# Memory keys and values of a two-part model made inside the expert loop, late norms' squares summed on GpSimd

## The reference

```python
def memory_cross_attention(h, mem_n, wq, wkv, wo, q_gain, k_gain):
    q = rms_norm((h @ wq).reshape(B_, T, X_HEADS, X_HEAD_DIM), q_gain)      # 4 heads of 256
    k, v = jnp.split(mem_n @ wkv, 2, axis=-1)
    k = rms_norm(k.reshape(B_, M, X_HEADS, X_HEAD_DIM), k_gain)
    ...
    return o @ wo
# in each layer l of the second block
x = x + 0.5 * swiglu(rms_norm(x, norm_ffn1[l]), ...)
x = x + concat(mixers of rms_norm(x, norm_mix[l])) @ w_out[l]
x = x + memory_cross_attention(rms_norm(x, norm_cross[l]), rms_norm(mem, norm_mem[l]), ...)
x = x + 0.5 * swiglu(rms_norm(x, norm_ffn2[l]), ...)
```

## Time and profile before

| | us |
|---|---|
| median of 3 runs (lowest, highest) | 3019.21 (3018.96, 3020.18) |
| the profiled execution | 3018.08 |
| its span, first to last instruction | 3016.5 |
| TensorE busy (matmul), share | 2541.1, 84% |
| VectorE, ScalarE, GpSimd busy | 1261.3, 874.6, 41.6 |
| read from DRAM, written | 659.21 MB, 1.05 MB |

### The profile page before, as it was taken

The page is one execution under the profiler, slowest core; times in us unless marked ns, Lnnn a source line. Parts: engine busy times, 40 slices in busy tenths (PEclk is TensorE's granted clock), DMA queues, the critical chain, the costliest instruction groups (busy, mean ns, idle before and its releaser), DMA issues.

```text
span 3016.5 us, 42653 instructions
## 1 busy us (share of the span) xinstructions
PE 2541.1 (84%) x18068; PEld 1984.1 (66%) x18068; DVE 1261.3 (42%) x1844; ACT 874.6 (29%) x1213; POOL 41.6 (1%) x52
## 2 busy tenths in 40 slices
PE   6898788666766767676999698989999997899999
PEld 6895384122212222223999587989999985888999
DVE  6665532000000000002656745655565566465555
ACT  3473021000000000002444422544444444144443
POOL 0000000000000000000000100000000001000000
PEclk9998897878777787777999788989999997899999
DMA  6443056999999999997554201425555540033453
GB/s 224 141 144 116 1 199 277 426 424 426 426 425 424 426 426 424 425 426 298 202 182 161 84 1 57 168 84 183 182 189 183 181 161 1 15 112 112 143 184 122
DMA packets 115400, 662.49 MB, mean 220 GB/s; under 512 B 10283, under 2 KB 12502, under 8 KB 57777
## 3 DMA queue, kind: packets, MB, share of 16 engines
q1 hardware_dynamic: 113376, 650.24, 55.4%
q0 software_dynamic: 1872, 10.06, 1.0%
HBM read 659.21 MB, written 1.05 MB: 219 GB/s over the span
## 4 chain that ended last, share of the span: by engine, by line
PE 60%; DMA 17%; DVE 10%; SPq 5%; DVEq 3%; ACT 3%; issue 2%; ACTq 0%; PEldq 0%; PEld 0%
PE psd L548 32%; PE psx L548 8%; DMA ring<-in_w_up 7%; SPq L2172 5%; DMA hx<-in_w_down 5%; DMA ring<-in_w_down 5%; PE psd L795 2%; PE psd L786 2%; PE psx L823 2%; PE psx L962 2%; DVE w_lo L1462 2%; PE psd L814 1%; DVE scr L1462 1%; PE psx L558 1%; PE psx L706 1%
## 5 line engine op out<-in xcount | busy, mean ns | idle before, releaser
L548 PE MATMUL psd<-h_hi,w_hi 128*128 128x256 f32 x2704 | 779.9, 288 | 43.8 <-DVE h_lo L1462 20.5
L548 PE MATMUL psd<-h_lo,w_hi 128*128 128x256 f32 x2704 | 773.4, 286 | 0.0
L548 PE MATMUL psd<-h_hi,w_lo 128*128 128x256 f32 x2704 | 773.0, 286 | 0.0
L1462 DVE TENSOR_TENSOR w_lo<-ring,w_hi 128x1024 fp32r<-128x1024 f32 (+1 forms) x468 | 550.1, 1217 | 492.3 <-ACT w_hi L1132 489.7
L1132 ACT ACTIVATE w_hi<-ring 128x1024 fp32r<-128x1024 f32 (+1 forms) x468 | 467.5, 1047 | 389.1 <-PE psd L548 383.7
L548 PEld LDWEIGHTS psd<-h_hi,w_hi 128*128 128x128 f32 x2704 | 527.8, 195 | 50.3 <-issue 24.7
L548 PEld LDWEIGHTS psd<-h_lo,w_hi 128*128 128x128 f32 x2704 | 527.7, 195 | 0.5
L548 PEld LDWEIGHTS psd<-h_hi,w_lo 128*128 128x128 f32 x2704 | 527.5, 195 | 0.0
L548 PE MATMUL psx<-halves,w_hi 128*128 128x256 f32 x1408 | 256.9, 284 | 3.2 <-issue 3.2
L548 PEld LDWEIGHTS psx<-halves,w_hi 128*128 128x128 f32 x1408 | 219.9, 192 | 4.2 <-issue 3.9
L1125 ACT ACTIVATE scr<-psd 128x512 f32<-128x512 f32 x56 | 33.2, 592 | 606.8 <-PE psd L801 316.8
(11 more groups left out here) (331 smaller groups left out, 3084.3 us busy)
## 6 DMA issues: line engine op xcount, KB each, us to landing
ring<-in_ffn_wi SPq DMA_DIRECT2D x88, 1024.0 KB, 4.8
scr<-in_w_gate SPq DMA_DIRECT2D x48, 1024.0 KB, 18.8
scr<-in_w_down SPq DMA_DIRECT2D x48, 1024.0 KB, 22.3
scr<-in_w_up SPq DMA_DIRECT2D x48, 1024.0 KB, 26.7
ring<-in_ffn_wo SPq DMA_DIRECT2D x44, 1024.0 KB, 4.8
ring<-in_w_gate SPq DMA_DIRECT2D x32, 1024.0 KB, 17.8
ring<-in_w_up SPq DMA_DIRECT2D x32, 1024.0 KB, 25.5
ring<-in_w_down SPq DMA_DIRECT2D x32, 1024.0 KB, 23.3
```

Of the source, the lines that this page charges most:

```text
L548: mm = pe.matmul(o, w[u], a[v], start=start and i == 0, stop=stop and i == 2, **kw)
L1462: return dve.tensor_tensor(o, a, b, op)
```

## The change

It does three things. The keys and values of both layers are made in the expert loop, one slot of `x_wkv` an expert: expert e of round `pair` makes slot `pair` of layer e; slots 0 to 3 are keys, 4 to 7 values. The matmuls are plain fp32 (16 a slot). Keys are normed in the loop. Results are stored to a DRAM tensor `kv` by ScalarE's queue and loaded again by GpSimd's queue in each layer. The memory is loaded, squared, summed and normed once, ahead of and at the start of the loop, mostly on GpSimd; `mem_n` lies in the buffers of x and sq, which are free during the loop. Second, `norm_cross` becomes a late norm, and both it and `norm_ffn2` are early. Third, the squares of late norms are summed by three adds on GpSimd from 8 tiles to 2, so TensorE does 2 matmuls.

```diff
# plan: x_k and x_v are gone, x_q is evicted by VectorE
-        after += [(("x_k", l), i, "x_wkv", (l, i)) for i in range(4)]
-        after += [(("x_v", l), i, "x_wkv", (l, 4 + i)) for i in range(4)]
# TensorE: norm, when g is a late norm
+                if g in SUMMED:
+                    pe.wait_ge(squares_summed, SUMMED.index(g) + 1)
+                    for k in range(2):
+                        mm = pe.matmul(b[:, 0:T], ones, squares_of.get(g, sq)[:, k, :], start=(k == 0), stop=(k == 1))
+                    done(mm)
+                    return
# TensorE: ffn's last step
-                                if g and dt in (3, 5):
-                                    norm(g, dt // 2 - 1, dt // 2)
# TensorE: expert, between the turns and "down"
                 pe.wait_ge(S("actT"), 2 * pair + e + 1)
+                pe.wait_ge(S("mem_normed"), 1)
+                pe.wait_ge(S("kv_w_landed"), 32 * pair + 16 * e + 16)
+                w = kv_w.rearrange("p (k c) -> p k c", k=KD)
+                for m in range(2):
+                    tile = slice(m * P, (m + 1) * P)
+                    for k in range(KD):
+                        a, b = (w[:, k, tile], mem_n[e][:, k, :]) if keys else (mem_n[e][:, k, tile], w[:, k, :])
+                        mm = pe.matmul(m2(psd[0])[:, m, :], a, b, start=(k == 0), stop=(k == KD - 1))
+                mm.then_inc(S("kv_made"), 1)
...
+                if keys:
+                    pe.wait_ge(S("k_squared"), 2 * pair + e + 1)
+                    for m in range(2):
+                        mm = pe.matmul(psd[1][:, 0:T], ones, k_sq[:, m, :], start=(m == 0), stop=(m == 1))
+                    mm.then_inc(S("k_summed"), 1)
                 pe.wait_ge(S("ye_ready"), 4 * pair + 2 * e + 2)
...
+                pe.wait_ge(S("kv_read"), 2 * pair + e + 1)
+                if keys:
+                    pe.wait_ge(S("k_root"), 2 * pair + e + 1)
# TensorE: cross-attention, after mix_out
                 for i in range(4):
-                    dense((("x_k", l), i), (mn_hi, mn_lo), f"norm_mem{l}" if i == 0 else None)
-                    if i == 1:
+                    dense((("x_q", l), i), (mn_hi, mn_lo), g=f"norm_cross{l}" if i == 0 else None)
+                    if i == 0:
                         norm(f"norm_cross{l}")
# TensorE: after cross-attention
-                then_norm(("x_o", l), f"norm_ffn2{l}", ("xo_cut", 4 * l), last=2)
-                ffn("ffn2", l, f"norm_ffn1{l + 1}" if l < LAYERS - 1 else None)
+                for i in range(4):
+                    dense((("x_o", l), i), (mn_hi, mn_lo), ready=None if i else ("xo_cut", 4 * l))
+                ffn("ffn2", l)
# ScalarE: expert, after actT
+                    act.wait_ge(S("kv_made"), 2 * pair + e + 1)
+                    if keys:
+                        act.activation(k_sq, m2(psd[0]), ACT.Square).then_inc(S("k_squared"), 1)
+                    act.wait_ge(S("kv_stage_free"), 32 * pair + 16 * e + 16)
+                    copy(kv_st, psd[0][:, :]).then_inc(S("kv_read"), 1)
                     act.wait_ge(slots_done, PAIR * pair + first + ESLOTS)
                     copy(ye[:, 0, :], psd[2][:, :]).then_inc(S("ye_ready"), 1)
+                    if keys:
+                        act.wait_ge(S("k_summed"), 2 * pair + e + 1)
+                        act.activation(k_rs, psd[1][:, 0:T], ACT.Sqrt, bias=eps_col,
+                                       scale=1.0 / 256).then_inc(S("k_root"), 1)
+                        act.wait_ge(S("k_scaled"), 2 * pair + e + 1)
...
+                    act.dma_start(kv[e, bass.ds(pair, 1), :, :].rearrange("a p c -> (a p) c"),
+                                  kv_st).then_inc(S("kv_stage_free"), 16)
# VectorE: x_q is multiplied by rstd; k_scaled: reciprocal of k_rs and two products in each key expert
+                for i in range(4):
+                    cut_ahead(cutter, (("x_q", l), i))
+                    b = m2(d_ready(dve, (("x_q", l), i)))
+                    dread(tt_(xq[:, 2 * i:2 * i + 2, :], b, by_token, ALU.mult))
# GpSimd
+            def sum_squares(g):
+
+                s, q = squares_of.get(g, sq), 4 * NORMS.index(g)
+                pool.wait_ge(sq_ready, q + 2)
+                pool.tensor_tensor(s[:, 0:2, :], s[:, 0:2, :], s[:, 2:4, :], ALU.add)
+                pool.wait_ge(sq_ready, q + 4)
+                pool.tensor_tensor(s[:, 4:6, :], s[:, 4:6, :], s[:, 6:8, :], ALU.add)
+                pool.drain()
+                pool.tensor_tensor(s[:, 0:2, :], s[:, 0:2, :], s[:, 4:6, :], ALU.add)
+                pool.drain().then_inc(squares_summed, 1)
...
+            load(mem[:, :, :], A["memT"].rearrange("(k p) t -> p k t", p=P), "mem_in")
+            DB.was_read(pool, ("w_b_out", 3))
...
+            for l in range(LAYERS):
+                for k in range(KD):
+                    pool.tensor_scalar(mem_n[l][:, k, :], mem[:, k, :], pc(f"norm_mem{l}", k), None, ALU.mult)
# SyncE, in the expert loop
                     expert_slot(s, pair)
+                    if s == 16 + ERING - 1:
+                        sp.wait_ge(S("kv_made"), 2 * pair + 1)
+                        kv_slot(1, pair)
+                    if s == ESLOTS + 16 + ERING - 1:
+                        sp.wait_ge(S("kv_made"), 2 * pair + 2)
+                        kv_slot(0, pair + 1)
```

More of the change, by code:

```diff
@@ L207, in dense_plan @@
         ffn(l, "ffn1")
-        for part, count, reader in (("mix_in", 11, "dve"), ("mix_out", 4, "dve"), ("x_k", 4, "act"),
-                                    ("x_v", 4, "act"), ("x_q", 4, "act"), ("x_o", 4, "dve")):
+        for part, count, reader in (("mix_in", 11, "dve"), ("mix_out", 4, "dve"), ("x_q", 4, "dve"),
+                                    ("x_o", 4, "dve")):
             plan += [(((part, l), i), reader) for i in range(count)]
@@ L246, in small_plan @@
     add("act", "norm", "g_ffn")
+    add("act", "norm_mem")
     add("dve", "router")
@@ L453, in program @@
         for l in range(LAYERS):
-            NORMS += [f"norm_ffn1{l}", f"norm_mix{l}", f"norm_mem{l}", f"norm_cross{l}", f"norm_ffn2{l}"]
+            NORMS += [f"norm_ffn1{l}", f"norm_mix{l}", f"norm_cross{l}", f"norm_ffn2{l}"]
         sq_ready, h_ready = S("sq_ready"), S("h_ready")
@@ L738, in _ @@
             then_norm("w_o", "g_ffn", ("merged", 0), (mn_hi, mn_lo))
+            b = XB.claim(pe, ("norm_mem",))
+            pe.wait_ge(S("mem_squared"), 1)
+            for i in range(2):
+                mm = pe.matmul(b[:, 0:T], ones, mem_sq[:, 0, i, :], start=(i == 0), stop=(i == 1))
+            done(mm)
             b = XB.claim(pe, ("router",))
@@ L778, in down_rows, with expert @@
                 return e_ring[s % ERING].rearrange("p (i c) -> p i c", i=2)
-            def expert(pair, e):
+            def expert(pair, e, keys):
                 first = e * ESLOTS
@@ L833, in _ @@
             for l in range(LAYERS):
-                if l == 0:
-                    norm(f"norm_ffn1{l}", 0, 2)
-                ffn("ffn1", l, f"norm_mix{l}")
+                ffn("ffn1", l)
                 for i in range(9):
@@ L1055, in _ @@
                 for i in range(4):
-                    dense((("x_k", l), i), (mn_hi, mn_lo), f"norm_mem{l}" if i == 0 else None)
-                    if i == 1:
+                    dense((("x_q", l), i), (mn_hi, mn_lo), g=f"norm_cross{l}" if i == 0 else None)
+                    if i == 0:
                         norm(f"norm_cross{l}")
[L1059 to L1080, removed]
                 b = XB.claim(pe, ("xnorm", l, "q", 0))
                 for hd in range(4):
-                    pe.wait_ge(S("x_sq"), 8 * l + 4 + hd + 1)
+                    pe.wait_ge(S("x_sq"), 4 * l + hd + 1)
                     for it in range(TT):
@@ L1175, in norm, with late_norm @@
                     cut_acts(h, hi, mid=mid)
-            def late_norm(g, part, l, first, early, each=None):
+            def late_norm(g, part, l, first, early, each=None, hi=h_hi):
                 for i in range(4):
@@ L1294, in _, with expert @@
                     read(copy(h_tok[:, tt, i * 512:(i + 1) * 512], b[:, :]))
-            with act.Fori(0, EXPERTS // 2) as pair:
-                for e in range(2):
+            act.drain().then_inc(S("kv_stage_free"), 16)
+            def expert(pair, e, keys):
                     first = MOE + e * ESLOTS
@@ L1791, in _, with expert @@
             dve.drain().then_inc(S("onehot"), 1)
-            def expert(pair, e):
+            XB.was_read(dve, ("norm_mem",))
+            dve.reciprocal(rmem, rmem).then_inc(S("mem_root"), 1)
+            for l in range(LAYERS):
+                tt_(k_gain[:, l, :], *(par[:, PCOL[f"x_{n}_gain{l}"]:PCOL[f"x_{n}_gain{l}"] + 2] for n in "qk"),
+                    ALU.mult)
+            def expert(pair, e, keys):
                 first = MOE + e * ESLOTS
@@ L1809, in expert @@
                 dve.tensor_copy(ye[:, 1, :], psd[3][:, :]).then_inc(S("ye_ready"), 1)
-            with dve.Fori(0, EXPERTS // 2) as pair:
-                for e in range(2):
```

(15 more changed lines are left out.)

169 lines of the change are left out of this document (88 added, 81 removed).

## The result

| | before | after |
|---|---|---|
| median, us (lowest, highest; runs) | 3019.69 (3018.96, 3021.63; 4) | 2971.68 (2968.78, 2974.15; 4) |
| the profiled execution, its span | 3018.08, 3016.5 | 2970.65, 2968.5 |
| read from DRAM, written, MB | 659.21, 1.05 | 662.36, 5.24 |
| GpSimd busy, us | 41.6 | 115.4 |

The changed kernel takes 0.9842 of the time (95% interval 0.9828 to 0.9857). The forecast was 2969 us.

The account below looks back on a forecast made before the run. The prediction took DMA to bound the expert loop and TensorE the dense stages: 3018.1 - 97.8 + 48.2 = 2968.5, with 1.1 to the median about 2969 us. Its own range was 2955 to 2983 (chance 0.57), the outer ends 2948 and 2995.

Parts of the forecast that it names:

- 15 weight slots: Expert loop: key and value weight slots added to the full DMA stream, 2.465 us each, cost 37.0 us.
- 16 stores: Expert loop: 256 KB stores of keys and values at the full stream's rate, 15 counted, cost 9.2 us (bounds 0 and 16.5).
- ahead of the loop: Before the expert loop: GpSimd's squaring of the memory touches VectorE's chain before w_o, costing 1 us.
- joint of x_q, layer 0: Dense joint: last slot's end through the late norm's two sum matmuls, 13.4 us, worked out at norm_ffn2.
- squares of q later, a layer: Cross-attention: last x_q is evicted after VectorE's weight cut and squared only then, costing 2.3 us a layer.
- norm_ffn2, a layer: Joint of x_o and feed-forward: early norm, 4 matmuls less among the slots (1.86) plus 2.4, gains 4.3 us a layer.
- lower clock behind it: Joint of x_q: after the idle TensorE runs 3.2 us at clock 0.51, costing 1.6 us.
- GpSimd's charge at a dense joint: Late norm: GpSimd's adds slow VectorE's low halves through the shared port, 1.0 us a joint (bounds 0 and 1.27+1.27).
- Rival 1: Loop and dense joints: stores ride free and joints carry no port or clock charges, 2950 us; chance 0.15.
- Rival 2: Expert loop: stream stumbles once per expert, SyncE late or stores holding loads, +39, 3008 us; chance 0.10, half of it 0.10 more.
- Rival 3: Expert loop: TensorE becomes the bound, deciding from mean clock 0.63; 3210 us at half clock; chance 0.03.
- Rival 4: Joints of x_q: the whole norm, root and reciprocal too, is exposed, 8 us a layer more, 2985 us; chance 0.05.

Follow-up runs that it names:

- e5: Against the changed kernel, every expert's key or value matmuls are done twice, the second time over the first: 2977.09 us.
- e6: Against the changed kernel, only the first slot of the keys' and values' weights is loaded and all 16 experts use it, SyncE's wait for kv_made removed: 2934.2 us.
- e3: Against the changed kernel, each expert's keys or values are stored a second time, to another DRAM tensor: 2982.64 us.
- e1: Against the changed kernel, the late norms' squares are summed on TensorE again (8 fp32 matmuls in place of 2), without GpSimd's adds: 2984.41 us.
- e4: Against the changed kernel, behind the last slot of mix_out, x_q and x_o the result leaves PSUM before the next weight slot is cut: 2942.93 us.

## Why the prediction was right

*The bound of each stage.* "A slot that moves from the dense stages into the expert loop gives back 5.76 us and costs 2.465" held: 43.8 and 44.9 us came back from the two cross-attention stages for 43.6 forecast, and the loop took +47.6 for 47.2. In all, 96.5 us came back behind the loop for 97.8, and 48.5 were paid for 48.2. e5 and e6 show the reason, not only the sum: compute doubled in the loop costs nothing but at its end, and weights left out of the stream give their time back.

*The terms against the runs:*

| step | forecast | measured |
|---|---|---|
| 15 weight slots | 37.0 | 38.3 (e6) |
| 16 stores | 9.2 | 9.35 (what e6 leaves), 9.8 (e3) |
| end of the loop | +1 | 0 (the last down slot waits 1.56 for DMA) |
| ahead of the loop | +1 | +0.9 (476.30 for 475.43), see below |
| joint of x_q, layer 0 | 13.4 | 13.5 |
| squares of q later, a layer | 2.3 | 1.4 and 1.2 |
| norm_ffn2, a layer | 4.3 | 3.2 and 3.3 |
| idle in the joint of x_q | 4.1 | 4.09 |
| lower clock behind it | 1.6 | 1.8 to 2.7 (e1) |
| GpSimd's charge at a dense joint | 1.0 | 0.1 to 0.7 on TensorE's path (e1), 0.9 on VectorE |
| first norm_ffn1 and three tails | 2 | 1.3 (what is left of the 96.5) |

Two of these agreements are luck. The 0.9 us ahead of the loop show nothing, since kernels that are the same up to there reach the first gather anywhere from 472.81 to 476.57. And in the dense joints two terms were off and made up for each other. In e1, where GpSimd is idle, the 36 matmuls behind the idle take 6.71 us at the joint of x_q (6.07 to 7.04 at the other three) for 4.32 at full clock, so the lower clock costs 1.8 to 2.7 and not 1.6. And GpSimd's 0.9 on VectorE lies mostly under those slow matmuls. The forecast's 1.6 is one stretch of 3.2 us at 0.51; in e1 the clock was 0.50 from 1933 to 1936 and still 0.66 from 1936 to 1939. The rows of the joint of x_q of the changed kernel, TensorE, VectorE and GpSimd:

```profile
1933.36 0.79 PE L549 MATMUL psd<-halves,w_hi 128*128 128x256 f32 x2 [4.09 <-DVE halves L1470]
```

```profile
1929.03 2.36 DVE L1470 TENSOR_TENSOR w_lo<-ring,w_hi 128x1024 fp32r<-128x1024 f32 x2 [1.49 <-ACT w_hi L1135]
...
1932.62 2.37 DVE L1470 TENSOR_TENSOR halves<-sq,halves 128x512 fp32r<-128x512 f32 x2
```

```profile
1932.73 1.71 POOL L2100 TENSOR_TENSOR scr<-scr 128x512 f32<-128x512 f32 x1 [9.79 <-ACT scr L1188]
1935.01 1.27 POOL L2102 TENSOR_TENSOR scr<-scr 128x512 f32<-128x512 f32 x1 [0.57 <-issue]
```

*norm_ffn2* is the step with a fault in its working, "4 matmuls less among these slots: 1.86 us". The code does them after the third and after the fourth slot, two and two. Only the first two stood between slots; the others ran behind the last slot, in the idle that follows. The chain of the kernel before has the one pair, and its timeline the second, at the end of the last slot (2010.93):

```profile
2004.31 0.86 PE psx L558 x4
```

```profile
2010.76 1.03 PE L558 MATMUL psx<-scr,con 128*128 128x256 f32 x4
```

From x_o's start to its end it took 22.72 us and takes 21.86: 0.86 saved, one pair. The joint itself gave the 2.4 forecast (15.84 to 13.5). I had counted instructions of a loop where I should have asked which of them stand on the path.

*The port.* The second add starts with the low halves and runs 1.71 us where it runs 1.27 alone (the third), and the two low halves take 2.37 for 1.47. The third add starts when they are done and meets nothing. So VectorE pays for one add, not for the two of my upper bound, and pays once: 0.9 us. The Trainium skill, "SBUF — State Buffer", section "SBUF: two separate sides", has the shared pair as a lock held for a whole instruction, the loser blocked. These rows agree in kind and not in size: both instructions grow, but VectorE's part of 1.47 and GpSimd's of 1.27, one after the other, would be 2.74, and the rows have both within 2.37 (1932.62 to 1934.99). The worst case of the prediction, 2.5 us a joint, does not arise, since only one add falls beside them.

*The rivals.* Rival 1 (stores free) falls by e3 and by the 9.35 us that e6 leaves. Rival 2 (SyncE late) falls by e6 and by SyncE's own waits. From 500 to 1400 us it waited for the keys' or values' matmuls (L825) once:

```profile
SPq L2236 <- PE psd L825: 2.4, 1, 2.4
```

That was at the first of them, which ended at 509.27; the load was issued at 509.45. Rival 3 (TensorE becomes the bound) needed a mean clock under 0.63; it rose to 0.83, and in e5 with 84 us more busy time to 0.86. Rival 4 (x_q exposes the whole norm) would have shown TensorE waiting for VectorE's reciprocal ahead of the second slot; the row at 1941.35 starts where the sum ends.

## What to carry to other kernels

Price work by the stage that it leaves and the stage that it enters: what moves under a stream that is the bound costs its bytes alone, loads and stores by the same rate, and its compute only where the stream ends. At a joint, the order of VectorE's queue is worth more than the work moved off TensorE: taking the result out before cutting the next weight gave 28.8 us for changes at five places, since TensorE idled less and its clock stayed at the upper level behind the shorter idle. And of each operation that a change removes ask where it ran: one that ran in an idle stretch gives nothing back.

## What the runs showed of the hardware

In the DMA-bound loop the granted clock was higher the more TensorE had to do: 0.78, 0.83 and 0.86 with 643, 731 and 815 us of busy time in 912 to 969. Right behind the added matmuls the others ran faster, further on they did not. The rows (line, instruction, count | busy us, mean ns | idle us before and its releaser) are "down" and "gate"/"up" of the kernel before, and then the same of the changed kernel:

```profile
L814 PE MATMUL psd<-scr 128*32 128x512 f32 x384 | 71.2, 882 | 35.0 <-DMA scr<-in_w_down 34.4
L795 PE MATMUL psd<-scr 128*32 128x512 f32 x768 | 124.7, 770 | 49.9 <-DMA scr<-in_w_up 44.8
```

```profile
L833 PE MATMUL psd<-scr 128*32 128x512 f32 x384 | 43.9, 595 | 4.0 <-DMA scr<-in_w_down 4.0
L805 PE MATMUL psd<-scr 128*32 128x512 f32 x768 | 134.3, 821 | 63.4 <-DMA scr<-in_w_up 58.2
```

"Down", which follows the added block, hardly waits for its slots any more and went from 882 ns to 595; "gate" and "up", which come later, went from 770 to 821.

In the dense joints the clock went with the length of the idle ahead. After the idle of 4.09 us and a burst of 6 matmuls it was 0.50, the lower level of 1.2 GHz, for 3 us. In e4, where the two idles around the same burst are short, it stayed at 1.00 (TensorE's timeline). All four joints agree: 30 matmuls take 5.44, 5.42, 5.10 and 5.41 us in the changed kernel and 3.86, 3.86, 3.85 and 3.85 in e4.

```profile
1925.39 0.50 PE L549 MATMUL psd<-halves,w_hi 128*128 128x256 f32 x2 [0.66 <-DVE halves L1471]
...
1927.08 0.50 PE L549 MATMUL psd<-halves,w_hi 128*128 128x256 f32 x2 [0.72 <-DVE halves L1471]
```
